# A hybrid encoder kernel on Trainium2: in the chunked delta-rule stage, VectorE does one doubling add after the result ops of the older job, not ahead of them

## The chip, the core and the metric

The kernel is one program on one core of a Trainium2 chip. The core has five engines that run side by side and meet at semaphores: TensorE (PE in the rows, its weight loads PEld), VectorE (DVE), ScalarE (ACT), GpSimd (POOL) and SyncE (SP), which issues DMAs. Each engine takes its own instructions in the order in which they are written. The metric is the device time of one execution in microseconds, lower is better; three runs of the kernel before gave 1784.24 us as their median (1783.65 to 1788.34).

## The reference

One encoder layer over 1024 tokens of width 1024: a projection into three head groups, an output projection, cross-attention into 256 memory tokens, a SwiGLU feed-forward and norms, all in float32. The stage that is changed belongs to the third head group, a bidirectional RWKV-7 mixer with 4 heads of 64, whose state is updated token by token:

```python
def step(S, inp):
    wt, kkt, kat, kt, vt, rt = inp
    S = (S * wt[..., None, :]
         - jnp.einsum('...vk,...k->...v', S, kkt)[..., :, None] * kat[..., None, :]
         + vt[..., :, None] * kt[..., None, :])
    return S, jnp.einsum('...vk,...k->...v', S, rt)

_, y = lax.scan(step, S0, xs)     # xs: both directions, the second one flipped in time
y = jnp.moveaxis(y, 0, 2)
y = y[0] + jnp.flip(y[1], axis=1)
```

## The kernel before

The scan is not run token by token. Time is cut into chunks of 64, two of which make a tile of 128 tokens. For a tile the kernel builds small 64x64 systems, inverts each of them by doubling, and gets from that a transition and an offset per chunk; only the chain over chunks is sequential. A tile in one direction is a job: 8 tiles in 2 directions make jobs 0 to 15 (direction 0 is jobs 0 to 7). A job takes one of three slots in turn (s_G, s_Q, s_LT, s_XQ and s_WU in the rows, with two PSUM banks each), so job g + 3 reuses the slot of job g.

Jobs are pipelined over steps p = 0 to 18. `jobs_at(p)` gives the job that enters (`new`, number p), the one of the step before (`mid`), the one before that (`old`) and the one whose results are ready (`done`). All four engines walk the same steps, each with its own order, written out by hand; nothing reorders it. For a job, the inverse has five rounds, 0 to 4: `new` does rounds 0 and (its first half) 1, `mid` the rest of 1, then 2 and 3, `old` round 4. A round is: TensorE transposes the running inverse Q (two matmuls, L2033) and multiplies it with the coupling block LT that GpSimd made (`xq`, 16 matmuls), ScalarE copies that to SBUF (L919), TensorE multiplies again (`inverse`, 16 matmuls), and VectorE adds the product to Q (`inverse`, L1461, one instruction, called the add here). After round 4 come `wu` and `results` on TensorE (80 small matmuls in `results`), and then `results(old)` on VectorE, four instructions (L1471, L1472, L1473, and L1476 for direction 0 or L1479 for direction 1). `add_y` (L1440) and `chain_step` (L1427, two instructions) belong to `done`.

TensorE's order in a step p, in the parts that matter, is: `xq(old, 4)`, `inverse(mid, 1)`, `gram(new)`, ..., `wu(old)`, `xq(mid, 3)`, `inverse(new, 0)`, `state_out(done)`, `results(old)`, `inverse(mid, 3)`, `xq(new, 1)`, `chain_step(done)`. The `mid` of one step is the `old` of the next, so the `xq(old, 4)` at the head of step p + 1 transposes what the add of `inverse(mid, 3)` of step p has written. `gram(new)` of step p + 1 writes the banks that `results(old)` of step p reads:

```python
def gram(j):                                   # TensorE, L1988
    pe.wait_ge(g_dve[j.i], j.dve0)             # VectorE is through with the slot's last job
...
def xq(j, l):                                  # TensorE, L2036
    pe.wait_ge(g_dve[j.i], j.dve0 + (DVE_Q[l - 1] if l else DVE_SYS))
    inverse_t(j)                               # the two transposes, L2033
```

In steps 1 to 7 VectorE also prepares the inputs of direction 1 piece by piece: `next(inputs1)` issues the next one or two instructions of `second_inputs()` (L1380 to L1419), `DVE_PREP` says how many of them a step has (4 or 5). GpSimd and ScalarE have such extra work in a few steps too. What follows the stage (group norm, output projection and all the rest) starts on every engine with a wait for the last `add_y`.

Of the kernel before, what the change touches and what calls it, by code (L numbers as in the profile page):

```python
# [55 lines left out]
def build(nc, io):  # L56
    out = io["out"]
    ctx = ExitStack()
    with ctx:
# [310 lines left out]
        def jobs_at(p):  # L370

            return [Job(p - age) if 0 <= p - age < 2 * NT else None for age in range(4)]
# [741 lines left out]
        def _(dve):  # L1114
# [327 lines left out]
            def gram(j):  # L1442
                sl = j.slot
                dve.wait_ge(g_pe[j.i], j.pe0 + PE_GRAM)
                for hp in range(2):
                    ins = TT(sl.G[:, :, hp:4:2, 0:2, :].rearrange("p a u r t -> p a u (r t)"),
                             PS[:, (sl.a, sl.b)[hp], :].rearrange("p (a u c) -> p a u c", a=2, u=2),
                             MK[:, j.d, 0:2 * C].unsqueeze(1).unsqueeze(1).broadcast_to([P, 2, 2, 2 * C]), ALU.mult)
                ins.then_inc(g_dve[j.i], 1)

            def system(j):
                sl, q = j.slot, j.slot.Q[:, :, :]
                dve.wait_ge(g_pe[j.i], j.pe0 + PE_SYS)
                link(TT(q.rearrange("p (a h) c -> p a h c", a=2), PS[:, sl.a:sl.b + 1, 0:2 * C].rearrange("p h (a c) -> p a h c", a=2),
                        MK[:, j.d, 2 * C:3 * C].unsqueeze(1).unsqueeze(1).broadcast_to([P, 2, 2, C]), ALU.mult))
                TT(q, q, I64.unsqueeze(1).broadcast_to([P, 4, C]), ALU.subtract).then_inc(g_dve[j.i], 1)

            def inverse(j, l):
                q = j.slot.Q[:, :, :].rearrange("p (a h) k -> p h a k", h=2)
                dve.wait_ge(g_pe[j.i], j.pe0 + PE_Q[l])  # L1460
                TT(q, PS[:, j.slot.a:j.slot.b + 1, 0:128].rearrange("p h (a k) -> p h a k", a=2), q, ALU.add).then_inc(g_dve[j.i], 1)  # L1461
# [20 lines left out]
            for p in range(STEPS):  # L1482
                new, mid, old, done = jobs_at(p)
                extra = DVE_PREP.get(p, 0)
                if mid:
                    inverse(mid, 1)
                if new:
                    gram(new)
                if extra > 4:
                    next(inputs1)  # L1490
                if old:
                    inverse(old, 4)
                if new:
                    system(new)
                if extra:
                    next(inputs1)
                if done:
                    if done.k == 0:
                        chain_first(done)
                    else:  # L1500
                        chain_step(done.d, 2 * done.k)
                if mid:
                    inverse(mid, 2)
                if new:
                    inverse(new, 0)
                if extra:
                    next(inputs1)
                if done:
                    add_y(done)
                if mid:  # L1510
                    inverse(mid, 3)
                if old:
                    results(old)
                if extra:
                    next(inputs1)
                if done and done.k < NT - 1:
                    chain_step(done.d, 2 * done.k + 1)
                if extra:
                    next(inputs1)
# [893 lines left out]
```

## Time and profile before

| what | value |
|---|---|
| median of three runs | 1784.24 us |
| the profiled execution, its own time | 1788.34 us |
| its span in the trace | 1786.5 us |
| TensorE busy | 1695.5 us (95%) |
| VectorE busy | 722.5 us (40%) |
| ScalarE busy | 665.0 us (37%) |
| GpSimd busy | 579.0 us (32%) |
| mean granted TensorE clock | 0.973 of full speed |

The profiled execution is one of the three timed. A row of a timeline gives the start in us from the start of the span, the time in us that the group of equal instructions took, engine, line, operation, what it writes and reads with the shapes, the number of instructions, and in brackets how long the engine was idle ahead of it and which instruction ended that. The ends of matmuls are modelled, as they are pipelined. Instructions of one engine overlap a little in the rows, because the next starts before the last one has drained. The stage goes from about 572 us to 783 us of the span, 12% of it.

### The profile page before, as it was taken

Reading aid. Unit: us, or ns where it says so; the run is one execution under the profiler, and the core shown is the slowest. Engines: PE = TensorE matmul, PEld = TensorE weight load, DVE = VectorE, ACT = ScalarE, POOL = GpSimd, SP = SyncE. Lnnn points to the kernel's source line nnn. Section 1 sums busy time; section 2 is a strip of 40 time slices with the busy share of each in tenths; the row PEclk is TensorE's granted clock in tenths of the full one; section 3 lists DMA queues with packets and bytes.
Section 4 is the critical chain, followed back from the end, with each engine's and each line's share of the span. In section 5 each row is a group of like instructions: output and inputs, shape, how many; then the busy total and the mean of one; then the engine's idle time right before and its main releaser. Section 6 shows DMA issues by size and latency. Waiting matters only on the chain.

```text
span 1786.5 us, 31965 instructions
## 1 busy us (share of the span) xinstructions
PE 1695.5 (95%) x13553; PEld 1398.7 (78%) x13553; DVE 722.5 (40%) x1223; ACT 665.0 (37%) x1244; POOL 579.0 (32%) x529
## 2 busy tenths in 40 slices
PE   6999999999876899989999999999999999999997
PEld 5887878788654677868888878888888888888886
DVE  3105888332165686653532641203303303312316
ACT  5225888423257444442554742211111212121112
POOL 5232663321035543355555013222222222212220
PEclk9999999999868899999999999999999999999999
DMA  6110000210000000016333012111111111111112
GB/s 195 48 64 6 1 1 1 66 48 12 18 1 6 3 4 4 5 43 237 98 107 108 7 42 60 49 53 48 48 47 54 42 47 54 47 42 58 49 42 94
DMA packets 62605, 87.44 MB, mean 49 GB/s; under 512 B 5010, under 2 KB 46128, under 8 KB 62464
## 3 DMA queue, kind: packets, MB, share of 16 engines
q1 hardware_dynamic: 61520, 82.89, 14.5%
q0 software_dynamic: 944, 2.52, 0.5%
q8 instruction: 108, 1.77, 0.4%
q14 instruction: 33, 0.27, 0.0%
HBM read 81.19 MB, written 4.19 MB: 48 GB/s over the span
## 4 chain that ended last, share of the span: by engine, by line
PE 86%; DVE 6%; ACT 4%; DMA 2%; POOL 1%; issue 1%; SPq 0%; ACTq 0%; DVEq 0%
PE PS L1701 13%; PE PS L1704 13%; PE PS L1702 13%; PE PS L1962 6%; PE PS L2333 4%; PE PS L2331 4%; PE PS L2332 4%; PE PS L1714 4%; PE PS L1716 4%; PE PS L1715 4%; PE PS L1806 3%; PE PS L1850 3%; PE PS L2033 2%; PE PS L1842 1%; PE PS L1740 1%
## 5 line engine op out<-in xcount | busy, mean ns | idle before, releaser
L480 POOL TENSOR_TENSOR WL<-RAW,WH 128x512 fp32r<-128x512 f32 x248 | 341.2, 1385 | 837.5 <-ACT WH L656 836.7
L1701 PE MATMUL PS<-HH,WH 128*128 128x512 f32 x1040 | 406.1, 391 | 0.3 <-DVE SM L1150 0.3
L1702 PE MATMUL PS<-HL,WH 128*128 128x512 f32 x1040 | 404.7, 389 | 0.0
L656 ACT ACTIVATE WH<-RAW 128x512 fp32r<-128x512 f32 x248 | 153.5, 631 | 558.8 <-PE PS L1704 275.2
L1704 PE MATMUL PS<-HH,WL 128*128 128x512 f32 x1040 | 325.5, 389 | 0.0
L1704 PEld LDWEIGHTS PS<-HH,WL 128*128 128x128 f32 x1040 | 195.2, 188 | 40.7
L1701 PEld LDWEIGHTS PS<-HH,WH 128*128 128x128 f32 x1040 | 195.3, 188 | 40.5 <-DVE SM L1150 0.4
L1702 PEld LDWEIGHTS PS<-HL,WH 128*128 128x128 f32 x1040 | 195.2, 188 | 40.0
L1651 DVE TENSOR_TENSOR FU<-PS,ACTB 128x512 f32<-128x512 f32 x44 | 27.3, 684 | 456.9 <-PE PS L1704 456.9
L2331 PE MATMUL PS<-WH,AH 128*128 128x512 f32 x352 | 136.9, 389 | 0.0
L2332 PE MATMUL PS<-WL,AH 128*128 128x512 f32 x352 | 136.9, 389 | 0.0
L2333 PE MATMUL PS<-WH,AL 128*128 128x512 f32 x352 | 136.9, 389 | 0.0
L1678 DVE TENSOR_TENSOR X<-PS,X 128x512 f32<-128x512 f32 x160 | 105.3, 686 | 60.1 <-PE PS L2333 60.1
L602 POOL TENSOR_TENSOR s_LT<-s_G,CN 128x256 f32<-128x256 f32 x80 | 60.4, 764 | 121.8 <-PE PS L1962 68.8
L1714 PE MATMUL PS<-WH,HH 128*128 128x512 f32 (+1 forms) x240 | 89.9, 374 | 3.8 <-POOL WL L480 3.8
L1201 DVE CUSTOM_DVE_ANT_0 E__70<-PS,TAB 128x1024 f32<-128x1024 f32 x64 | 78.2, 1225 | 30.8 <-PE PS L1806 29.9
L1716 PE MATMUL PS<-WH,HL 128*128 128x512 f32 (+1 forms) x240 | 88.0, 367 | 0.0
L1715 PE MATMUL PS<-WL,HH 128*128 128x512 f32 (+1 forms) x240 | 87.8, 366 | 0.0
L754 ACT ACTIVATE E__70<-E__70,SM 128x1024 f32<-128x1024 f32 x64 | 73.6, 1151 | 21.0 <-DVE SM L1201 20.8
L919 ACT ACTIVATE s_XQ<-PS 128x512 f32<-128x512 f32 (+1 forms) x80 | 51.2, 640 | 78.0 <-PE PS L1962 78.0
L2333 PEld LDWEIGHTS PS<-WH,AL 128*128 128x128 f32 x352 | 66.1, 188 | 13.7
L2331 PEld LDWEIGHTS PS<-WH,AH 128*128 128x128 f32 x352 | 66.1, 188 | 13.7
(349 smaller groups left out, 2713.1 us busy)
## 6 DMA issues: line engine op xcount, KB each, us to landing
RAW<-in_ffn_w_gu SPq DMA_DIRECT2D x88, 256.0 KB, 2.8
RAW<-in_w_in SPq DMA_DIRECT2D x48, 256.0 KB, 2.7
RAW<-in_ffn_w_down SPq DMA_DIRECT2D x44, 256.0 KB, 2.5
RAW<-in_w_out SPq DMA_DIRECT2D x32, 256.0 KB, 2.8
XT<-in_x SPq DMA_DIRECT2D x8, 512.0 KB, 5.5
X<-in_x SPq DMA_DIRECT2D x8, 512.0 KB, 6.4
RAW<-in_x_wq SPq DMA_DIRECT2D x16, 256.0 KB, 2.7
RAW<-in_x_wkv SPq DMA_DIRECT2D x16, 256.0 KB, 2.6
```

Of the source, the lines that this page charges most:

```text
L480: pool.tensor_tensor(w_low, RAW[:, p % NRAW], w_high.bitcast(F32), ALU.subtract).then_inc(w_lo, 1)
L656: act.activation(split_at(p)[0], RAW[:, p % NRAW], ACT.Copy).then_inc(w_hi, 1)
L1701: pe.matmul(where(ct, i), wh[:, k, c], ah(kt)[:, t0:t0 + n], start=first and starts(ct, i), stop=False, skip_group_check=True)
L1702: pe.matmul(where(ct, i), wh[:, k, c], al(kt)[:, t0:t0 + n], start=False, stop=False, skip_group_check=True)
L1704: mm = pe.matmul(where(ct, i), wl[:, k, c], ah(kt)[:, t0:t0 + n], start=False, stop=last, skip_group_check=True)
L1714: pe.matmul(dst, ah(kt)[:, t], wh, start=start, stop=False, skip_group_check=True)
L1715: pe.matmul(dst, ah(kt)[:, t], wl, start=False, stop=False, skip_group_check=True)
L1716: return pe.matmul(dst, al(kt)[:, t], wh, start=False, stop=last, skip_group_check=True)
L1962: return pe.matmul(dst, lhsT, rhs, start=start, stop=stop, skip_group_check=True)
L2331: pe.matmul(PS[:, bank, :], AH[:, a, t], wh, start=k == 0, stop=False, skip_group_check=True)
L2332: pe.matmul(PS[:, bank, :], AH[:, a, t], wl, start=False, stop=False, skip_group_check=True)
L2333: return pe.matmul(PS[:, bank, :], AL[:, a, t], wh, start=False, stop=k == 1, skip_group_check=True)
```

## The change

On VectorE, `inverse(mid, 3)` moves from ahead of `results(old)` to behind it and behind the `next(inputs1)` that follows. No other engine's code is touched.

```diff
--- before.py
+++ after.py
@@ -1507,12 +1507,12 @@
                     next(inputs1)
                 if done:
                     add_y(done)
-                if mid:
-                    inverse(mid, 3)
                 if old:
                     results(old)
                 if extra:
                     next(inputs1)
+                if mid:
+                    inverse(mid, 3)
                 if done and done.k < NT - 1:
                     chain_step(done.d, 2 * done.k + 1)
                 if extra:
```

The sequences of TensorE, ScalarE, GpSimd and SyncE are the same in both programs. On VectorE, step p = 8 stands like this before, from `add_y` to the mask ops of the next step (KR, BKt: keys of direction 0; YY: the output; g_pe0 to g_pe2: TensorE's semaphore of a slot):

```order
L1440 TENSOR_TENSOR YY<-PS,YY 128x2x128 [waits y_mm]
L1461 TENSOR_TENSOR s_Q<-PS,s_Q 128x2x2x64 [waits g_pe1]
L1471 TENSOR_TENSOR KR<-PS,KR 128x2x128 [waits g_pe0]
L1472 TENSOR_TENSOR BKt<-PS,CN 128x2x128
L1473 TENSOR_TENSOR BKt<-PS,SM 128x2x128
L1476 COPY YY<-PS 128x2x128
L1427 SCALAR_TENSOR_TENSOR KR<-PS,SM,BKt 128x64 [waits c_mm]
L1427 SCALAR_TENSOR_TENSOR KR<-PS,SM,BKt 128x64
L1461 TENSOR_TENSOR s_Q<-PS,s_Q 128x2x2x64 [waits g_pe2]
L1446 TENSOR_TENSOR s_G<-PS,MK 128x4x128 [waits g_pe0]
```

The first L1461 here is the add of `inverse(mid, 3)`, the second that of `inverse(mid, 1)` of step 9. VectorE's step p = 8 in the program after:

```order
L1440 TENSOR_TENSOR YY<-PS,YY 128x2x128 [waits y_mm]
L1471 TENSOR_TENSOR KR<-PS,KR 128x2x128 [waits g_pe0]
L1472 TENSOR_TENSOR BKt<-PS,CN 128x2x128
L1473 TENSOR_TENSOR BKt<-PS,SM 128x2x128
L1476 COPY YY<-PS 128x2x128
L1461 TENSOR_TENSOR s_Q<-PS,s_Q 128x2x2x64 [waits g_pe1]
L1427 SCALAR_TENSOR_TENSOR KR<-PS,SM,BKt 128x64 [waits c_mm]
L1427 SCALAR_TENSOR_TENSOR KR<-PS,SM,BKt 128x64
L1461 TENSOR_TENSOR s_Q<-PS,s_Q 128x2x2x64 [waits g_pe2]
L1446 TENSOR_TENSOR s_G<-PS,MK 128x4x128 [waits g_pe0]
```

The add has moved behind the four ops of `results(old)`. Steps 8 to 16 are alike, but for L1479 in place of L1476 from step 10 on. In step p = 4 (and alike in 2, 3, 5, 6 and 7) VectorE has an op of `second_inputs()` there as well, here an L1402, which the add moves past too:

```order
 L1440 TENSOR_TENSOR YY<-PS,YY 128x2x128 [waits y_mm]
-L1461 TENSOR_TENSOR s_Q<-PS,s_Q 128x2x2x64 [waits g_pe0]
 L1471 TENSOR_TENSOR KR<-PS,KR 128x2x128 [waits g_pe2]
 L1472 TENSOR_TENSOR BKt<-PS,CN 128x2x128
@@ -523,4 +523,5 @@
 L1476 COPY YY<-PS 128x2x128
 L1402 TENSOR_TENSOR B__113<-B__113,ET 128x512
+L1461 TENSOR_TENSOR s_Q<-PS,s_Q 128x2x2x64 [waits g_pe0]
 L1427 SCALAR_TENSOR_TENSOR KR<-PS,SM,BKt 128x64 [waits c_mm]
 L1427 SCALAR_TENSOR_TENSOR KR<-PS,SM,BKt 128x64
```

In step p = 1 VectorE has no `old`, and the add moves past one call of `next(inputs1)` alone, which there is two instructions:

```order
 L1461 TENSOR_TENSOR s_Q<-PS,s_Q 128x2x2x64 [waits g_pe1]
 L1383 SCALAR_TENSOR_TENSOR KR_112<-SCM,KR_112 128x512
+L1386 TENSOR_SCALAR SM<-KR_112 128x16 [waits dve_chain]
+L1388 TENSOR_TENSOR KR_112<-KR_112,SM 128x512 [waits dve_chain]
 L1461 TENSOR_TENSOR s_Q<-PS,s_Q 128x2x2x64 [waits g_pe0,dve_chain]
-L1386 TENSOR_SCALAR SM<-KR_112 128x16
-L1388 TENSOR_TENSOR KR_112<-KR_112,SM 128x512 [waits dve_chain] x2
+L1388 TENSOR_TENSOR KR_112<-KR_112,SM 128x512
 L1461 TENSOR_TENSOR s_Q<-PS,s_Q 128x2x2x64 [waits g_pe1,dve_chain]
```

The second L1461 of this piece is the add; L1386 and the first L1388 now stand ahead of it.

## Rows read from the trace of the kernel before

**Rows 1.** Windows: stretch, its length, busy time of each engine, PEclk, DMA, GB/s
```profile
687.31:763.64 76.33, 76.25 (x2673) 62.65 (x2673) 46.98 (x125) 34.66 (x63) 25.26 (x35) 1.00 0.02 5
640.80:644.20 3.40, 1.58 (x41) 0.97 (x40) 3.40 (x8) 0.95 (x2) 1.24 (x3) 1.00 0.00 0
644.20:647.60 3.40, 3.40 (x64) 2.51 (x68) 2.79 (x7) 1.85 (x4) 1.38 (x2) 0.58 0.02 5
```

**Rows 2.** Timeline of VectorE around the add of step p = 8
```profile
687.31 0.42 DVE L1461 TENSOR_TENSOR s_Q<-PS,s_Q 128x256 f32<-128x256 f32 x1 [1.21 <-PE PS L1962]
...
688.98 0.47 DVE L1427 SCALAR_TENSOR_TENSOR KR<-PS,SM,BKt 128x64 f32<-128x64 f32 x2
```

**Rows 3.** Timeline of TensorE, from the last matmul of results in p = 8
```profile
686.78 0.22 PE L1962 MATMUL PS<-s_G,s_WU 64*64 64x64 f32 x1
686.78 0.45 PE L1962 MATMUL PS<-s_XQ 64*64 64x64 f32 x15
...
688.14 0.44 PE L2033 MATMUL PS<-CN,s_Q 128*128 128x128 f32 x2
...
688.79 0.41 PE L1962 MATMUL PS<-s_XQ 64*64 64x64 f32 x16
689.11 0.67 PE L1962 MATMUL PS<-KR,B__113 64*64 64x128 f32 x16
```

**Rows 4.** Timeline of both engines at the end of step p = 16
```profile
771.93 0.42 DVE L1461 TENSOR_TENSOR s_Q<-PS,s_Q 128x256 f32<-128x256 f32 x1 [1.21 <-PE PS L1962]
...
772.41 0.44 PE L2033 MATMUL PS<-CN,s_Q 128*128 128x128 f32 x2 [0.33 <-DVE s_Q L1461]
```

**Rows 5.** Timelines of VectorE and of TensorE after step p = 5
```profile
652.01 0.42 DVE L1461 TENSOR_TENSOR s_Q<-PS,s_Q 128x256 f32<-128x256 f32 x1 [0.64 <-PE PS L1962]
...
653.68 0.68 DVE L1411 TENSOR_TENSOR KR<-KR,KK 128x512 f32<-128x512 f32 x1
...
655.60 1.28 DVE L1446 TENSOR_TENSOR s_G<-PS,MK 128x512 f32<-128x512 f32 x2
...
652.85 0.44 PE L2033 MATMUL PS<-CN,s_Q 128*128 128x128 f32 x2
...
653.82 1.10 PE L1962 MATMUL PS<-KR,BKt 64*64 64x128 f32 x32
```

**Rows 6.** Timelines of VectorE, GpSimd and TensorE after step p = 4
```profile
639.27 2.15 DVE L1402 TENSOR_TENSOR B__113<-B__113,ET 128x512 f32<-128x512 f32 x1
641.35 0.46 DVE L1427 SCALAR_TENSOR_TENSOR KR<-PS,SM,BKt 128x64 f32<-128x64 f32 x2
...
642.82 1.27 DVE L1446 TENSOR_TENSOR s_G<-PS,MK 128x512 f32<-128x512 f32 x2
...
638.52 2.36 POOL L592 TENSOR_TENSOR B__113<-B__113,KK 128x1024 f32<-128x1024 f32 x1
...
638.54 0.44 PE L2033 MATMUL PS<-CN,s_Q 128*128 128x128 f32 x2
...
639.19 0.41 PE L1962 MATMUL PS<-s_XQ 64*64 64x64 f32 x16
639.42 1.10 PE L1962 MATMUL PS<-KR,BKt 64*64 64x128 f32 x32
```

**Rows 7.** Timelines of VectorE and of TensorE after step p = 1
```profile
597.42 0.52 DVE L1386 TENSOR_SCALAR SM<-KR 128x16 f32<-128x16 f32 x1
597.98 1.42 DVE L1388 TENSOR_TENSOR KR<-KR,SM 128x512 f32<-128x512 f32 x2
...
597.56 0.44 PE L2033 MATMUL PS<-CN,s_Q 128*128 128x128 f32 x2 [0.49 <-DVE s_Q L1461]
...
598.88 1.10 PE L1962 MATMUL PS<-KR,BKt 64*64 64x128 f32 x32 [0.26 <-ACT B__113 L830]
```

**Rows 8.** Timeline of TensorE after step p = 2 and after step p = 7
```profile
614.47 0.70 PE L1962 MATMUL PS<-s_Q,s_LT 64*64 64x64 f32 x16 [0.68 <-POOL s_LT L602]
...
678.22 0.67 PE L1962 MATMUL PS<-KR,B__113 64*64 64x128 f32 x16 [1.21 <-issue]
```

## The prediction

> **What bounds the kernel now.** I count the stage in steps p, as the code does; the add is VectorE's op of L1461 for `inverse(mid, 3)`, which starts at 652.01 us in p = 5, at 687.31 in p = 8 and at 771.93 in p = 16 [rows 2, 4, 5].
>
> First I read the windows by stage. From p = 8 to p = 15 TensorE is busy for 76.25 of 76.33 us at the full clock [rows 1], and VectorE for 46.98. Seven steps fit in, 10.9 us each, so a hole that is newly made in TensorE's row there is added to the time. Before p = 8 VectorE is the busier engine and TensorE waits at places.
>
> Second, the timelines of both engines at one steady step. VectorE finishes `add_y`, sits idle for 1.21 us, and at 687.31 does the add, 0.08 us after the last matmul that makes its input (686.78 + 0.45 = 687.23). The four ops of `results(old)` follow, then `chain_step` at 688.98 [rows 2]. That looks like a hole to fill, since the input of `results(old)` was complete at 686.78 + 0.22 = 687.00 [rows 3], 0.23 us sooner.
>
> Third, who needs these two. TensorE runs `inverse(mid, 3)`, `xq(new, 1)`, `chain_step`, and then, as the first work of the next step, the two transposes (L2033, 688.14) of the block that the add writes. Two groups later comes `gram(new)`, at 689.11, which reuses the slot that `results(old)` reads [rows 3]. The add is therefore needed first, at 688.14, and now ends 0.41 us before (687.31 + 0.42 = 687.73). `results(old)` is needed second: its last op started at 688.98 - 0.33 = 688.65, and its end some 0.4 us later, about 689.05, is just ahead of the start of `gram`.
>
> **The change, part by part.** No instruction is added or removed on any engine, one add moves behind four ops, and in p = 1 to 7 also behind one op of `second_inputs()`. In p = 0 and 17 to 18 nothing moves. 16 steps have a `mid`, p = 1 to 16.
>
> *p = 8 to 15.* Five starts from 687.31 to 688.98 make 0.334 us an op [rows 2]. Now `results(old)` starts at 687.31 - 0.23 = 687.08, the add at 687.08 + 4 x 0.334 = 688.42, and it ends at 688.84. TensorE starts about 0.06 us after such an end (771.93 + 0.42 = 772.35, then 772.41 [rows 4]), at 688.90 instead of 688.14: a stall of 0.76 us. What is queued behind it on TensorE is everything: `inverse(mid, 1)`, `gram`, the transposes of the keys. One thing comes back: `gram` waited for `results(old)` a little, since a group of 16 such matmuls that nobody holds is followed after 0.23 us (639.42 - 639.19 [rows 6]) and here after 0.32 (688.79 to 689.11 [rows 3]). So 0.76 - 0.09 = 0.67 us a step. The seven steps p = 8 to 14 give 4.7 us. In p = 15 there is no `gram` behind: 0.76.
>
> *p = 16.* TensorE already waits here for the add, [0.33 <-DVE] at 772.41 [rows 4]. The add moves by 4 x 0.334 - 0.23 = 1.11 us, and the last chain of `xq`, `inverse`, `wu`, `results` hangs on it: 1.11.
>
> *p = 3, 5, 6.* One op of `second_inputs()` goes ahead as well. At p = 5: the add starts at 652.01 - 0.23 + 1.34 + 0.60 = 653.72 (0.60 is the 0.68 us of the op at 653.68 less the 0.08 by which ops in a row overlap, 0.42 long and 0.334 apart), ends at 654.14, and TensorE goes on at 654.20 instead of 652.85, 1.35 late, 1.26 at `gram`. But here VectorE got to the mask ops of the next step (L1446) only at 655.60; TensorE's `gram` ended at 654.92, and will end at 656.18, so that VectorE starts 0.06 later, at 656.24: 0.64 us of the 1.26 is seen [rows 5]. Steps 3 and 6 have the same rows, at p = 3 with a longer extra op: 3 x 0.64 = 1.9.
>
> *p = 4.* VectorE has no idle ahead of the add here, so `results(old)` takes its place, and the extra op (L1402) starts one op sooner, 639.27 - 0.33 = 638.94. That op took 2.15 us at 639.27, and a GpSimd op of 2.36 us lay beside it from 638.52 to 640.88 [rows 6]. If it always takes its 2.08 us from start to start, the add starts at 641.02, TensorE resumes 0.48 us later, at 641.50 instead of 638.54, `gram` ends at 640.52 + 2.96 = 643.48, and VectorE's mask op starts at 643.54 instead of 642.82: 0.72. If it is held until the GpSimd op ends, it is over no sooner than before, and the add starts at 641.35: 1.05. Lower bound 0.7, upper 1.1; I take 1.0, as this row is the only one of its kind that is that long and its end follows GpSimd's. The Trainium skill says of this (SBUF — State Buffer, section "SBUF: two separate sides") that a VectorE op with two SBUF inputs and a GpSimd op exclude each other on a shared port for the whole instruction; by that rule the term is 1.05, without it 0.72, and the trace leans to the rule with 2.15 us against 0.68 for an op of the same size at 653.68 [rows 5].
>
> *p = 1.* No `old` yet, two small ops go ahead (L1386 and one L1388): 0.56 + 0.71 = 1.27 us. TensorE waits for the add at 597.56 already, but at 598.88 it waited for ScalarE. The way from the transposes to `gram` takes 0.65 us (688.14 to 688.79 [rows 3]) and 0.23, so it would have been ready at 598.44, and 0.44 is slack [rows 7]: 0.83.
>
> *p = 2 and 7.* After p = 2 the next release of TensorE is GpSimd's, at 614.47 [rows 8]. TensorE's stall is large, since a scan goes ahead of the add, yet GpSimd's work doesn't move with it: 0.1, at worst 0.5. After p = 7 TensorE stood at `gram` for 1.21 us, for a small VectorE op that now comes 0.2 us sooner [rows 8]; the stall of 1.35 fills that hole: 0, between -0.2 and +0.2.
>
> *The clock.* In 640.80 to 644.20 TensorE was busy for 1.58 us and in the next 3.40 us its granted clock was 0.58, that is mostly 1.2 GHz [rows 1]. One such stretch costs at most 0.42 x 3.4 = 1.4 us. The holes made here have 0.7 us in the steady part; the forecast keeps the present number of slow stretches (bounds: one fewer, -1.4; three more, +4.3).
>
> *Sum:* 0.83 + 0.1 + 1.9 + 1.0 + 0 + 4.7 + 0.76 + 1.11 = 10.4 us. On the profiled execution (1788.34, span 1786.5) that is 1798.7. That execution was the slowest of the three shown, 4.1 above the median, with nothing to say that the stage caused it, so I put the sum on the median: 1784.24 + 10.4 = **1794.6**. What follows the stage starts from the last `add_y` on all engines, so nothing later can take it back.
>
> **The rivals.**
> *Not slower.* VectorE is the bound, and its idle 1.21 us is now partly used. Then each of the 15 steps with both jobs ends 0.23 us sooner: -3.5, 1780.8. For it: VectorE is fully busy from 640.80 to 644.20 [rows 1]. It decides if TensorE needs the doubling add at least 1.1 us after it is now done; at p = 8 it has 0.41 us [rows 2, 3], so this fails at each step. Chance 0.03.
> *The early steps hide it.* Only p = 8 to 16 counts, as the waits of p = 1 to 7 swallow the rest: 4.7 + 0.76 + 1.11 = 6.6, 1790.8. For it: TensorE was busy for 1.58 of 3.40 us there [rows 1]. Against: the slack was subtracted above. Chance 0.09.
> *More slow clock early.* The holes of 1.3 to 3.3 us in p = 1 to 6 drop the clock in up to three more steps: +4.3, 1798.9. For it: the row of 0.58. Against: the hole of 1.21 us after p = 7 [rows 8] was followed by none, the clock being 1.00 from p = 8 on. Chance 0.14.
> *The clock alternates in every step.* 14 stretches of 1.4: +20, 1814.6. The 76 us at full clock have no hole of this kind, so rows neither show nor exclude it; holes up to 1.2 us without a fall speak against it. Chance 0.03. The Trainium skill speaks for this one: TensorE: Matmul & The Clock Gate, section "A second HAM failure mode: psum-queue depth-cycling", tells of a kernel in which short idles between groups of matmuls came often enough for the clock to swing. No row of this trace shows that.
>
> **How the numbers follow.** The forecast has 0.71, with its own range 1791.5 to 1797.5 (terms of p = 1, 2, 4 and 7 at their bounds, one slow stretch either way, half a microsecond for the median itself). The four rivals have the other 0.29. The range of eight in ten takes in the early-hiding case at the low end and the three stretches at the high end: 1790 to 1800. A measurement of this kernel can tell about 0.3%, 5.4 us, so 1789.6 is the border. All cases but the first rival lie above it, the second by 1.2 us only, half a term: slower 0.94, within 0.05, faster 0.01.
>
> **What would show it.** In the new trace TensorE's transposes L2033 at the head of each step carry an idle of about 0.7 us released by DVE L1461, and a steady step lasts 11.55 us instead of 10.89. VectorE's idle before L1461 there falls from 1.21 us to nothing, and a shorter one of about 1.0 us stands before L1471. From the start of p = 8 to that of p = 15 it is 81.0 us instead of 76.3. Wrong would be a steady step that stays at 10.9 us, TensorE's next wait being on `gram`, or a granted clock under 1.00 between p = 8 and 15.

## The result

The changed kernel takes 1804.86 us (median of 4 runs, 1802.16 to 1805.86), the kernel before 1784.63 in the same comparison: ratio 1.0107, interval 1.0089 to 1.0126. The forecast was 1794.6 with a range of 1790 to 1800. The direction was right, the time was 10 us too low and outside the range.

The comparison flatters the kernel before. In the later comparisons, up to both_fill, it ran 97 more times between 1782.5 and 1797.9, median 1789.2 (17 more beside combo have 1788.1). The four times above, of which three are those that I started from, lie for the most part at the low end of that spread. One further execution of it, 2150.4 us, has no trace and is left out. A second comparison of the changed kernel gave 1804.5 (6 runs, 1799.5 to 1808.0) beside 1789.5, ratio 1.0078, interval 1.0059 to 1.0097. So the change costs 14 to 15 us, not 20, where the forecast's sum had 10.4.

### The profile page after: what moved, and what is told of

It is laid out like the page before. It is cut to its first block, busy times and chain, and to the rows that moved or that the text cites. A ratio compares the mean times of both kernels' runs of the same rounds, so it can differ in the third digit from the quotient of the medians.

```text
span 1798.0 us, 31966 instructions
## 1 busy us (share of the span) xinstructions
PE 1692.0 (94%) x13553; PEld 1396.2 (78%) x13553; DVE 720.9 (40%) x1223; ACT 666.0 (37%) x1244; POOL 577.1 (32%) x529
## 4 chain that ended last, share of the span: by engine, by line
PE 86%; DVE 7%; ACT 4%; DMA 1%; issue 1%; POOL 1%; SPq 0%; ACTq 0%; DVEq 0%
PE PS L1701 13%; PE PS L1704 13%; PE PS L1702 13%; PE PS L1962 7%; PE PS L2333 4%; PE PS L2331 4%; PE PS L2332 4%; PE PS L1714 4%; PE PS L1716 4%; PE PS L1715 4%; PE PS L1806 3%; PE PS L1850 3%; PE PS L2033 2%; PE PS L1842 1%; PE PS L1740 1%
## 5 line engine op out<-in xcount | busy, mean ns | idle before, releaser
L602 POOL TENSOR_TENSOR s_LT<-s_G,CN 128x256 f32<-128x256 f32 x80 | 60.4, 763 | 132.5 <-PE PS L1962 67.8
L1714 PE MATMUL PS<-WH,HH 128*128 128x512 f32 (+1 forms) x240 | 89.6, 373 | 3.1 <-POOL WL L480 3.0
L2332 PEld LDWEIGHTS PS<-WL,AH 128*128 128x128 f32 x352 | 66.1, 188 | 13.7
L2331 PEld LDWEIGHTS PS<-WH,AH 128*128 128x128 f32 x352 | 66.1, 188 | 13.7
```

Source lines behind the costliest of these rows:

```text
L1714: pe.matmul(dst, ah(kt)[:, t], wh, start=start, stop=False, skip_group_check=True)
L2331: pe.matmul(PS[:, bank, :], AH[:, a, t], wh, start=k == 0, stop=False, skip_group_check=True)
L2332: pe.matmul(PS[:, bank, :], AH[:, a, t], wl, start=False, stop=False, skip_group_check=True)
```

## The profile after, against the rows of before

Windows of the changed kernel, one for each of the steps p = 1 to 5 (each from the first mask op L1446 of a step to that of the next) and one for p = 8 to 14. Columns are length, busy time of TensorE, its weight load, VectorE, ScalarE and GpSimd, then the granted clock, the DMA share and GB/s.

```profile
583.26:596.17 12.91, 9.87 (x243) 6.94 (x244) 9.23 (x14) 5.97 (x9) 4.25 (x5) 0.96 0.01 3
596.17:610.47 14.30, 11.89 (x353) 9.31 (x354) 10.43 (x18) 4.93 (x9) 12.23 (x11) 0.86 0.01 3
610.47:628.83 18.36, 14.53 (x377) 12.02 (x378) 12.06 (x23) 9.18 (x13) 10.24 (x10) 0.78 0.01 3
628.83:642.90 14.07, 11.10 (x385) 9.16 (x386) 11.07 (x23) 4.96 (x9) 10.72 (x9) 0.98 0.01 4
642.90:655.27 12.37, 10.81 (x385) 8.88 (x385) 9.46 (x22) 7.80 (x13) 3.60 (x5) 1.00 0.02 4
...
679.85:760.18 80.33, 75.33 (x2681) 61.81 (x2676) 47.44 (x124) 34.69 (x63) 25.23 (x35) 1.00 0.02 5
```

In the steady part TensorE was busy for 76.25 of 76.33 us [rows 1], and is now for 75.33 of 80.33, at the full clock both times. The new 4 to 5 us are holes, and nothing else changed there. In p = 1 and 2 the granted clock is below 1; before, it was 1.00 in both. Before, it was low in p = 3 (0.69) and p = 5 (0.87) instead. Length times missing clock, summed over p = 1 to 7, is about 6.8 us in this trace as in that of before; in after_again it is 8.4, in early 9.8.

Timelines of VectorE and of TensorE in step p = 8 (the bracket is the engine's idle time just before the row and what released it):

```profile
687.93 0.42 DVE L1471 TENSOR_TENSOR KR<-PS,KR 128x256 f32<-128x256 f32 x1 [0.98 <-PE PS L1962]
688.27 0.41 DVE L1472 TENSOR_TENSOR BKt<-PS,CN 128x256 f32<-128x256 f32 x1
688.60 0.41 DVE L1473 TENSOR_TENSOR BKt<-PS,SM 128x256 f32<-128x256 f32 x1
688.93 0.41 DVE L1476 COPY YY<-PS 128x256 f32<-128x256 f32 x1
689.26 0.42 DVE L1461 TENSOR_TENSOR s_Q<-PS,s_Q 128x256 f32<-128x256 f32 x1
...
688.67 0.40 PE L1962 MATMUL PS<-KR,BKt 64*64 64x64 f32 x8
689.74 0.44 PE L2033 MATMUL PS<-CN,s_Q 128*128 128x128 f32 x2 [0.67 <-DVE s_Q L1461]
```

This is the predicted picture of [rows 2] and [rows 3]: the idle of 1.21 us ahead of the add is now 0.98 ahead of L1471, and TensorE stands for 0.67 us until the add is done. The sum had 0.76 for this wait. The steady step is 11.49 us instead of 10.89; seven of them differ by 4.0 us.

The last step with an add, p = 16, answers to [rows 4]:

```profile
779.10 0.44 PE L2033 MATMUL PS<-CN,s_Q 128*128 128x128 f32 x2 [1.42 <-DVE s_Q L1461]
```

0.33 us of waiting has become 1.42, 1.09 more; the forecast had 1.11.

Step p = 5, for [rows 5], VectorE, GpSimd and TensorE:

```profile
651.58 0.42 DVE L1476 COPY YY<-PS 128x256 f32<-128x256 f32 x1
651.91 0.97 DVE L1411 TENSOR_TENSOR KR<-KR,KK 128x512 f32<-128x512 f32 x1
652.80 0.41 DVE L1461 TENSOR_TENSOR s_Q<-PS,s_Q 128x256 f32<-128x256 f32 x1
...
655.27 1.29 DVE L1446 TENSOR_TENSOR s_G<-PS,MK 128x512 f32<-128x512 f32 x2 [0.45 <-PE PS L1962]
...
651.61 0.72 POOL L602 TENSOR_TENSOR s_LT<-s_G,CN 128x256 f32<-128x256 f32 x1 [2.32 <-PE PS L1962]
...
653.27 0.44 PE L2033 MATMUL PS<-CN,s_Q 128*128 128x128 f32 x2 [1.56 <-DVE s_Q L1461]
```

The mechanism is the forecast's: the stall is passed on through `gram`, and VectorE then waits 0.45 us for it. But the op L1411 now starts while GpSimd's L602 is running (651.61 to 652.33) and takes 0.97 us where it took 0.68, so that it ends 0.55 us after L602. Its place in time had changed, and I had priced it at its old duration.

Step p = 4, for [rows 6]:

```profile
638.12 2.38 DVE L1402 TENSOR_TENSOR B__113<-B__113,ET 128x512 f32<-128x512 f32 x1
640.42 0.41 DVE L1461 TENSOR_TENSOR s_Q<-PS,s_Q 128x256 f32<-128x256 f32 x1
...
637.62 2.34 POOL L592 TENSOR_TENSOR B__113<-B__113,KK 128x1024 f32<-128x1024 f32 x1
...
640.89 0.44 PE L2033 MATMUL PS<-CN,s_Q 128*128 128x128 f32 x2 [2.97 <-DVE s_Q L1461]
```

L1402 ends at 640.50, 0.54 us after GpSimd's op; before, it ended 0.54 after it as well (641.42 and 640.88). Against GpSimd's op it started 0.25 us earlier and took 0.23 us longer. The Trainium skill's rule (SBUF — State Buffer, section "SBUF: two separate sides"), under which the term was 1.05 instead of 0.72, is borne out: the step takes 14.07 us instead of 13.01 (14.00 in both_fill, at the full clock).

Steps p = 1 and p = 2 are where the picture differs, TensorE at [rows 7] and [rows 8]:

```profile
593.78 0.44 PE L2033 MATMUL PS<-CN,s_Q 128*128 128x128 f32 x2 [1.90 <-DVE s_Q L1461]
...
594.66 1.46 PE L1962 MATMUL PS<-KR,BKt 64*64 64x128 f32 x32
596.05 1.11 PE L2007 MATMUL PS<-CN,BKt 128*128 128x128 f32 x4
...
607.76 0.44 PE L2033 MATMUL PS<-CN,s_Q 128*128 128x128 f32 x2 [2.41 <-DVE s_Q L1461]
...
608.64 1.78 PE L1962 MATMUL PS<-KR,BKt 64*64 64x128 f32 x32
610.35 1.11 PE L2007 MATMUL PS<-CN,BKt 128*128 128x128 f32 x4
```

Behind these two holes of 1.9 and 2.4 us the clock falls to its low level (granted 0.50 from 596 to 598 and from 610 to 612 us), and it falls on `gram` (1.46 and 1.78 us for what takes 1.10, row 598.88 in [rows 7]) and on the transposes of the keys (1.11; 0.66 at 655.14, at the full clock). VectorE waits for that `gram`. A long hole alone does not bring the low clock about: the holes of 2.97 us in p = 4 and 1.56 in p = 5 left it at 0.98 and 1.00 in this trace. The forecast had let the number of slow stretches stand; I had not asked where they would lie.

The end of the stage, from the last add (L1461 in p = 17) to the end of the last `add_y`, has the same instructions in both programs. Windows of it, before and changed:

```profile
774.49:783.04 8.55, 4.67 (x152) 3.78 (x148) 3.93 (x13) 0.98 (x2) 0.00 (x0) 1.00 0.01 4
781.18:791.36 10.18, 6.54 (x152) 5.67 (x148) 3.93 (x13) 0.98 (x2) 0.00 (x0) 0.75 0.01 3
```

It takes 1.6 us longer, at a granted clock of 0.75 instead of 1.00; in after_again and late it is 10.5 us. The forecast priced nothing here. The low clock stands behind the new wait of 1.42 us at L2033, but that this wait brings it about is not shown: one_op, in which the add moves by 0.10 us only, has 10.5 too.

Last, the work behind the stage, which the prediction left out. TensorE in the kernel before, then in the changed one:

```profile
783.10 3.70 PE L2143 MATMUL PS<-YY,CN 128*128 128x512 f32 x8 [0.53 <-DVE YY L1440]
787.76 3.70 PE L2143 MATMUL PS<-CIN,CN 128*128 128x512 f32 x8 [0.96 <-DVE CIN L1524]
792.02 4.37 PE L1869 MATMUL PS<-CN,SQY 128*128 128x2 f32 x32 [0.55 <-ACT SQY L976]
796.25 0.77 PE L1714 MATMUL PS<-WH,HH 128*128 128x512 f32 x1
```

```profile
791.42 6.24 PE L2143 MATMUL PS<-YY,CN 128*128 128x512 f32 x8 [0.53 <-DVE YY L1440]
797.49 3.60 PE L2143 MATMUL PS<-CIN,CN 128*128 128x512 f32 x8
801.98 5.74 PE L1869 MATMUL PS<-CN,SQY 128*128 128x2 f32 x32 [0.89 <-ACT SQY L976]
807.59 0.77 PE L1714 MATMUL PS<-WH,HH 128*128 128x512 f32 x1
```

No instruction differs here, yet from L2143's start to the first L1714 it is 13.15 us before and 16.17 now, since the first group (L2143) took 6.24 us instead of 3.70 and L1869 5.74 instead of 4.37, with a granted clock of 0.61 from 791.42 to 798 us. The profiled execution is 1800.18 us, 12 more than that of before (1788.34); the stage itself, from the first mask op to the end of its last `add_y`, is 13.5 us longer (209.5 to 223.0: 6.1 in p = 1 to 7, 4.0 in p = 8 to 14, 3.5 from p = 15 on), this stretch 3.0, and the first part of the kernel happened to be 5.2 shorter, by its granted clock (0.89 instead of 0.84 from 400 to 560 us).

## The experiments

All were timed beside the kernel before on the same chip. The times in us that the first expectations name stand on a kernel before of 1784.6; it had 1789.1 beside them, so the differences are what to compare. Extra lines shift the line numbers: L2033 of before is L2035 or L2037 in some runs, L2143 is L2153. The length of each step, read from the starts of L1446, in us:

| kernel | p=1 | 2 | 3 | 4 | 5 | 6 | 7 | 8 to 14 | ratio (interval) |
|---|---|---|---|---|---|---|---|---|---|
| before | 11.59 | 13.18 | 16.59 | 13.01 | 12.78 | 11.39 | 12.39 | 76.34 | 1 |
| changed | 12.91 | 14.30 | 18.36 | 14.07 | 12.37 | 12.39 | 12.59 | 80.33 | 1.0107 |
| changed again | 13.16 | 14.37 | 17.09 | 15.53 | 13.56 | 12.38 | 12.60 | 80.34 | 1.0078 (1.0059 to 1.0097) |
| early | 13.09 | 14.39 | 17.06 | 15.36 | 12.37 | 13.34 | 14.14 | 77.35 | 1.0059 (1.0038 to 1.0080) |
| late | 11.59 | 13.17 | 16.59 | 13.00 | 12.78 | 11.39 | 12.39 | 81.37 | 1.0032 (1.0016 to 1.0049) |
| early_res | 11.60 | 12.93 | 15.58 | 13.03 | 11.38 | 11.49 | 12.16 | 78.66 | 0.9990 (0.9976 to 1.0004) |
| early_extra | 13.06 | 13.45 | 15.80 | 12.34 | 10.95 | 11.46 | 11.82 | 78.06 | 0.9990 (0.9973 to 1.0007) |
| after_fill | 12.54 | 13.11 | 17.14 | 14.01 | 12.56 | 12.42 | 12.60 | 82.51 | 1.0055 (1.0038 to 1.0072) |
| both_fill | 12.53 | 13.10 | 17.16 | 14.00 | 12.40 | 12.45 | 12.86 | 83.56 | 1.0043 (1.0027 to 1.0060) |

**before_again: the kernel before, once more.** 

> The kernel before, once more, for a second trace. The first trace of it lasted 1788.3 us and the median of its runs is 1784.6. If executions differ by where TensorE's clock falls (the first trace has 0.50 to 0.54 in 572.8 to 586.4 and 0.5 in 613.6 to 623.8), this trace lasts about 1784 us and has fewer or shorter stretches under 1.00 up to the end of the scan stage, with the steps p = 8 to 15 at 10.9 us as before. If the 4 us were something else (DMA, a longer launch), the stretches are the same.

1788.49 us, and each step of p = 1 to 7 within 0.02 us of the first trace. The expectation of another clock pattern was a miss: the same steps (p = 3 at 0.69, p = 5 at 0.87) are slow again.

**early and late: the change in p = 1 to 7 alone, and in p = 8 to 16 alone.**

```
early:                                   late:
-                if mid:                 -                if mid:
+                if mid and p >= 8:      +                if mid and p < 8:
                     inverse(mid, 3)                          inverse(mid, 3)
                 (results, extra)                         (results, extra)
+                if mid and p < 8:       +                if mid and p >= 8:
+                    inverse(mid, 3)     +                    inverse(mid, 3)
```

> The add is moved in steps p = 1 to 7 alone, and stands where it did from p = 8 on. The prediction's terms for these steps give 0.83 + 0.1 + 1.9 + 1.0 = 3.9 us: 1788.5. If the holes made in TensorE there also lower its granted clock (the trace after has 0.69 to 0.81 in p = 1 to 4), the time is 6 us or more above before, 1790.5 to 1794, and the steps p = 1 to 4 together are at least 4 us longer than before.

> The add is moved in steps p = 8 to 16 alone. Order alone: 7 steps of 0.6 (as measured in the trace after), 0.76 and 1.11, together 6.1 us: 1790.7. If the clock is what made the rest, the time is above that only by what falls at the end of the stage (granted 0.60 at 783.6 to 787.0 and 0.5 at 804 to 811 in the trace after): up to 3 us more, 1793.7. If early and late parts add up to the whole +20 us, neither part alone can be near these sums, and late would be at 1796 or more.

late: 1794.62 us, 5.7 above the kernel before, where the forecast's terms for p = 8 to 16 give 6.6. early: 1798.85, 10.5 above by its ratio, where the terms give 3.9. So the later part came out near its sum and the early one did not. The two add up to 16, against 14 to 19 for the whole. That late came out near is partly luck: its steady steps take 5.0 us more than before instead of 4.7, and the end of the stage is 2.0 longer, which the sum had at nothing, so that its trace is 8.8 us longer from p = 1 on.

**one_op and late_three: the dose.** The add stands behind one of the four ops of `results` (p = 2 to 16), or behind three of them (p = 8 to 16).

```
                 TT(g, rm[:, :, :, 0, :], g, ALU.add)
+                if between:          # one_op: here; late_three: two ops on
+                    between()
```

> The add is put behind the first of the four result ops (L1471) in steps p = 2 to 16, and stands as before in p = 1. By the order theory what counts is how much later the add ends than TensorE needs it: it had 0.41 us ahead, less 0.06 for the semaphore, and now moves by 0.334 - 0.23 = 0.10 us, so TensorE doesn't wait in the steady steps, and gram, which waited 0.09 us for the results, is released 0.23 us sooner: the steady step is 10.80 us instead of 10.89, and the whole is between -2 and 0 us against before, 1782.6 to 1784.6. If any op ahead of the add costs (a theory by which the position itself matters, not the time), it is slower by 0.3 us a step, about +5.

> In p = 8 to 16 the add goes behind three of the four ops of results(old), and nothing changes in p = 1 to 7. The steady step was 10.89 us with the add first, about 10.9 behind one op, 11.49 behind four. By the forecast's working (0.334 us an op, a slack of 0.41 + 0.23 us, 0.09 back at gram): 0.334 less than with four, 11.16 us. If the step were set by something that all orders but the first share, it would be 11.49 here too.

one_op took 1787.56 us, ratio 0.9988 (0.9973 to 1.0003): no loss, and a gain that is not told from nothing. Its steady steps are 10.85 us at best, not the expected 10.80, and some have gaps (11.47, 11.53). late_three, one execution, has undisturbed steady steps of 11.16 to 11.18 us, as its expectation worked out; with the add first they are 10.89, behind four ops 11.49. The fourth op costs 0.32 us and one op costs nothing: the slack, and 0.33 us for an op behind it, are shown in the length of the step.

**after_again: the changed kernel beside the parts.** 

> The changed kernel once more, timed beside the kernel before on this chip. The parts run alone gave +10.5 us (p = 1 to 7) and +5.7 (p = 8 to 16), together 16. Theory A, the parts add up: ratio 1.009, 15 to 18 us above the kernel before. Theory B, the first difference of 20 us came from a kernel before that was timed in a low moment (1784.6 against 1789.1 later): 10 to 13 us, as the forecast's sum had it (10.4). The steady steps are 11.49 us again under both.

Ratio 1.0078, between the two expectations: the parts add up within the intervals (14 by this ratio, 19 by the first, 16 by the parts), and 10 us lies just outside the interval (10.6 to 17.4).

**early_res: in p = 2 to 7 the add behind `results`, but ahead of the extra op.** 

> In p = 2 to 7 the add goes behind results(old) but stays ahead of the op of second_inputs(); p = 1 and p = 8 to 16 are as before. It divides the +10.5 us of the early part. If the loss is the four ops of results(old) (1.11 us a step, in six steps, less what is hidden): +4 to +7 us. If it is the op of second_inputs() that goes ahead (0.6 to 2.1 us a step, and it drags a GpSimd op along): 0 to +3 us here, and the rest, 7 us or more, comes with that op.

```
-                if mid:
+                if mid and p >= 8:
                     inverse(mid, 3)
                 if old:
                     results(old)
+                if mid and p < 8:
+                    inverse(mid, 3)
                 if extra:
```

0.9990 (0.9976 to 1.0004): it costs 0.7 us at most, where 4 to 7 had been expected if the four ops were the loss. Its trace has TensorE waiting for the add behind each of p = 2 to 7 (0.93, 0.67, 0.72, 0.67, 0.67 and 0.67 us), and the steps no longer for it, but for 0.1 in p = 6: `gram` is late by less than VectorE's own lead.

**early_extra: the extra op first, then the add, then `results`.** 

> In p = 1 to 7 the op of second_inputs() goes ahead of the add, and results(old) behind both; p = 8 to 16 are as before. The add behind results(old) alone cost nothing (0.999), behind both it cost 10.5 us. Theory threshold: VectorE is the bound of these steps and absorbs a late gram up to about 0.7 us; one op ahead of the add (0.6 us, 2.1 in p = 4) stays under that but in p = 4, as the four ops alone (1.1 us) did, and only both together pass it: 0 to +3 us. Theory that the loss is the order of the op of second_inputs() itself, by what it drags along on GpSimd: +6 us or more here too.

```
-                if mid:
+                if mid and p >= 8:
+                    inverse(mid, 3)
+                if extra:
+                    next(inputs1)
+                if mid and p < 8:
                     inverse(mid, 3)
                 if old:
                     results(old)
-                if extra:
-                    next(inputs1)
```

0.9990 as well (0.9973 to 1.0007). Four ops alone cost nothing, the extra op alone costs nothing, both together cost 10.5 us (early, 7 to 14 by its interval). That is a threshold, as the forecast's subtraction at p = 5 had it (1.26 us late at `gram`, 0.64 of it seen), and it speaks against a loss that the extra op brings along by itself on GpSimd. Single steps do change: p = 1, which is as in early, is 1.5 us longer than before, p = 4 and 5 are 0.7 and 1.8 shorter.

**early_567: the change in p = 5, 6 and 7 alone.** 

> The add goes behind results(old) and the op of second_inputs() in p = 5, 6 and 7 alone. The forecast had 0.64, 0.64 and 0 for these: +1.3 us. The traces of the changed kernel have 12.38 us for a full-clock step p = 5 or 6 where 11.38 would be free of any wait: +1.0 each and some 0.3 in p = 7, together +2.3. If most of the +10.5 us sat here: +5 or more; otherwise p = 1 to 4 carry some 6 to 8 us, where the forecast had 2.6.

```
-                if mid:
+                if mid and p not in (5, 6, 7):
                     inverse(mid, 3)
                 (results, extra)
+                if mid and p in (5, 6, 7):
+                    inverse(mid, 3)
```

1792.78 us, ratio 1.0020 (1.0000 to 1.0040), 3.6 us with an interval of 0 to 7. It holds both 1.3 and 2.3 and cannot tell them apart; in its trace p = 6 and 7 are 1.0 and 0.2 us longer than before. The greater part of the early loss seems to be left for p = 1 to 4.

**after_fill: the changed kernel with matmuls in the new holes.** 

> The changed kernel, with five extra matmuls (128 x 128, result unused) on TensorE at the end of p = 1 to 6, where it waits for the moved add. They fill about 1.1 us of the wait and change no order of the real work. If the early loss is granted clock lost behind the new holes: 3 to 6 us faster than the changed kernel, and no window of p = 1 to 7 under 0.9. If it is the waits themselves: within 2 us of the changed kernel, and the slow windows may go without any gain.

```
+                if 1 <= p <= 6:
+                    for _ in range(5):
+                        pe.matmul(PS[:, FRONT, 0:128], ID, ID, start=True, stop=True, ...)
```

The result of these matmuls is unused; they are called filler below. 1800.82 us, 4 less than the changed kernel beside it, though the intervals of the two ratios (1.0038 to 1.0072 here, 1.0059 to 1.0097 there) overlap. p = 1, 2 and 4 are at the full clock, as windows of its successor both_fill show:

```profile
586.11:598.64 12.53, 10.80 (x253) 7.90 (x254) 9.23 (x14) 5.97 (x9) 4.25 (x5) 1.00 0.01 3
598.64:611.74 13.10, 11.52 (x363) 9.26 (x363) 11.01 (x18) 4.93 (x9) 11.41 (x10) 1.00 0.01 4
611.74:628.90 17.16, 14.77 (x387) 12.27 (x388) 11.89 (x24) 9.17 (x13) 11.28 (x11) 0.80 0.01 3
628.90:642.90 14.00, 12.36 (x395) 10.20 (x395) 11.50 (x22) 4.96 (x9) 10.67 (x9) 1.00 0.02 4
```

The same steps took 12.91 to 13.16, 14.30 to 14.39 and 14.07 to 15.53 us in the three traces without filler. The clock's part of these steps is the difference, 0.4 to 0.6, 1.2 to 1.3 and 0.1 to 1.5 us. (In early, p = 6 and 7 are slow as well, at 0.92 and 0.86.) What is left against before is the wait alone: 0.94, -0.08 and 0.99 us, where the forecast had 0.83, 0.1 and 1.0. Of its expectation's window under 0.9 one stayed, in p = 3, where the hole is another one.

**tail_fill, before_tail: matmuls in the waits of p = 18, in the changed kernel and in the one before.**

```
+                if p == STEPS - 1:
+                    fill(6, FRONT)       # ahead of chain_step; 2 ahead of state_out, 2 at the end
```

> The changed kernel, with ten extra matmuls (results unused) on TensorE in the last step of the stage, p = 18, where it waits 1.8, 0.6 and 0.5 us; nothing real is moved. In the traces of the changed kernel the 8 matmuls of L2143 behind the stage took 6.2 to 6.8 us and those of L1869 5.2 to 5.7, against 3.70 and 4.4 to 4.7 before; from the last add_y to the first matmul of the next projection it is 16.2 us against 13.2 to 13.7. If the holes of that last step set the clock there: 16.2 becomes 13 or less and the time 2 to 4 us shorter. If not: 16.2 stays, and the time is that of the changed kernel.

> The kernel before with the ten extra matmuls in p = 18 alone. It tells whether they pay only where the changed order had lost the clock: two traces of the kernel before had 13.2 and 13.7 us behind the stage, and 12.4 is to be had, so 0 to 1 us under the kernel before. If the stretch behind the stage is slow in many of its executions too (its times spread over 15 us): 2 to 3 us under it, and the filler in the changed kernel corrected nothing that the change had done.

TensorE behind the stage in tail_fill:

```profile
796.67 3.70 PE L2153 MATMUL PS<-YY,CN 128*128 128x512 f32 x8
801.34 3.70 PE L2153 MATMUL PS<-CIN,CN 128*128 128x512 f32 x8 [0.97 <-DVE CIN L1524]
805.48 3.73 PE L1869 MATMUL PS<-CN,SQY 128*128 128x2 f32 x32 [0.44 <-ACT SQY L976]
809.08 0.70 PE L1714 MATMUL PS<-WH,HH 128*128 128x512 f32 x1
```

16.2 us became 12.4, and the changed kernel's ratio 1.0051 (1.0032 to 1.0070), 1798.66 us. But the kernel before gains as well: 1785.75, ratio 0.9980 (0.9962 to 0.9997), 0.5 to 6.8 us. Its trace has 12.7 us there, where the two traces of before have 13.2 and 13.7, which alone would be a gain of 0.5 to 1.0. So other executions of before may have the stretch slow; no trace of it does. early_res, as fast as before, has it slow (16.2). The difference of the two kernels with this filler is 12.9 us, against 14 to 15 without. I had taken the stretch for a loss of 3 us by the change, and this control takes 1 to 2 of them back.

**both_fill: both fillers in the changed kernel.** 

> The changed kernel with both fillers: five extra matmuls at the end of p = 1 to 6 and ten in p = 18 (results unused). Alone, the one left 1800.8 us with a slow clock behind the stage (16.2 us to the next projection), the other 1798.7 with a slow clock in p = 1, 2 and 4. If clock is what the forecast lacked: both together lie at the forecast's waits, 10 us above the kernel before or less (7 to 10), with 12.4 us behind the stage and 12.5, 13.1 and 14.0 us in p = 1, 2 and 4. If the fillers gain nothing together beyond the better one: 10 to 12 us.

1798.52 us, ratio 1.0043: 7.7 us above before, within the expected 7 to 10, but no better than tail_fill alone, and 12.8 above before_tail, which was timed beside it. So it does not show that the waits of the forecast are all that is left at the full clock. Against tail_fill its trace has won 5.3 us in p = 1 to 7 and lost 2.9 in p = 8 to 14. There TensorE stood once in each of the seven steps inside or at the end of a group of `results` (0.19 us, then 0.58 to 0.71) for nothing that the profile shows:

```profile
700.75 0.21 PE L1962 MATMUL PS<-s_G,s_WU 64*64 64x64 f32 x1 [0.65 <-issue]
```

The two traces of before, the two of the changed kernel and that of tail_fill have no such gap in p = 8 to 14; late has none either; the other ten have one to four. They are one reason for 82 or 83 us where seven undisturbed steps take 80.3. The extra matmuls may add to them; this was not tried apart.

**best_fill: early_res with matmuls in p = 0 to 6 and 18.** 

> The version that might beat both: in p = 2 to 7 the add behind results(old) only, p = 8 to 16 as before, and extra matmuls (results unused) in TensorE's waits: 5 and 7 in p = 0, 3 at the end of p = 1 to 6, 10 in p = 18. At equal mean granted clock the early order cost nothing; the filler can win what slow stretches cost in p = 0 to 7 and behind the stage, 8 to 14 us of slow clock in the traces, of which at most half is worth time: 3 to 7 us under the kernel before. If the clock is not tied to these waits: within 1 us of it.

1788.99 us, ratio 0.9993 (0.9978 to 1.0008): a miss. The granted clock rose from a mean of 0.976 to 0.982 and p = 0 to 7 took 100.3 us instead of 105.8, but steady steps with gaps (12.25 us, 11.52) and the stretch behind the stage (14.6) gave it back in the trace. A clock that is kept up in waits is not time won.

**combo: early_extra, one_op for p = 8 to 16, and the filler of p = 18.** 

> The parts that cost nothing or gained, together: in p = 1 to 7 the op of second_inputs() first, then the add, then results(old); in p = 8 to 16 the add behind the first of the four ops of results(old); and the ten extra matmuls in p = 18 (results unused). Alone they stood at 0.9990, 0.9988 and 0.9980. If they add: 0.996, 6 to 8 us under the kernel before. If the first two are no gain at all, as their intervals allow: 0.998, 3 to 4 us under it.

1782.51 us (12 runs, 1778.20 to 1784.97), ratio 0.9965, interval 0.9949 to 0.9981. It beats both kernels, at the low edge of what was expected (5.6 us by the medians, 6.3 by the ratio). Since before_tail alone has 0.9980, the two orders are worth some 2 to 3 us together by the ratios, which their intervals do not tell from nothing. Its undisturbed steady steps are 10.75 to 10.77 us, shorter than the 10.89 of before.

## Why the prediction was wrong

**The mechanism was right.** TensorE, not VectorE, needs the add at the head of each step; the hole on VectorE was no slack. The signs of the steady part came as named: 0.67 us of idle at L2033 released by L1461, 11.49 us a step (forecast 11.55), 0.98 us ahead of L1471 (about 1.0), 80.3 us for seven steps (81.0), granted clock 1.00.

**The waits, term by term** (forecast, measured at the full clock): p = 1 0.83, 0.94; p = 2 0.1, -0.1; p = 4 1.0, 1.0; p = 5 and 6 0.64 each, 1.0 each (12.37 and 12.39 against 11.38 in early_res and 11.39 in before); p = 7 0, 0.2 (for its hole of 1.21 us the row names "issue", not the small VectorE op that I named); p = 8 to 14 4.7, 4.0; p = 15 and 16 1.87, 1.84 (the add of p = 16 starts 18.05 us behind the mask op of p = 15 instead of 16.21). p = 3 cannot be had free of the clock. With 1.0 for it, as for its likes p = 5 and 6, which is an assumption, the sum is 10.9, and the forecast had 10.4. Two waits were mis-sized: that of p = 5 and 6 by 0.35 us each, 0.3 of which is what L1411 takes longer beside GpSimd, and the steady one, 0.57 us a step where I had 0.67. That the two errors nearly cancel, +0.7 and -0.7 us, is luck. One reading was wrong without effect on the sum: before p = 8 VectorE is not the busier engine (70.5 us against 81.1 of TensorE in p = 1 to 7 of before). The rival that VectorE gains, the one in which the early steps hide everything, and the alternating clock in the steady part are refuted: the change costs time, early costs 10.5 us, and the steady clock is 1.00 with a hole of 0.67 us in each step. For the last one the Trainium skill had spoken (TensorE: Matmul & The Clock Gate, "A second HAM failure mode: psum-queue depth-cycling"); holes of this kind do not bring it about here.

**What failed, first step: "I put the sum on the median: 1784.24".** Three runs gave 1783.65 to 1788.34, and I allowed half a microsecond for it. The kernel's usual time is 1789.2 (median of 97 runs), with a standard deviation of 3.6. This is 5.0 of the 10.3 us by which the time was missed. The changed kernel had 1804.86 in the first comparison and 1804.5 in the second, so it was the times of before that lay low, and not the whole comparison. I had also argued the profiled 1788.34 away as the slow one of three; it was the ordinary one.

**Second step: "the forecast keeps the present number of slow stretches", the clock put at nothing.** In the traces p = 1 to 7 together are longer than before by 6.1 us (changed kernel), 7.8 (after_again) and 8.8 (early). The waits above make 5.0 of it, with the assumed 1.0 for p = 3, so 1.0, 2.7 and 3.8 are left for the clock. The slow time had hardly grown in the first of them (6.8 us both times); it had moved onto `gram`, for which VectorE waits. The end of the stage, in which nothing moved, adds 1.6 to 2.0 us at a clock of 0.66 to 0.75. For the changed kernel that is 2.6 to 4.7 us where the forecast had 0. With the 5.0 of the base and 0.5 of the waits it makes 8.1 to 10.2 of the 10.3 us.

The rival "more slow clock early", to which I gave 0.14, comes nearest: holes of 1.9 to 3.0 us were being made next to the rows in which a short idle stretch was followed by 0.58. But it expected more slow steps, where the first trace has the same slow time in other places, and the end of the stage was in no rival.

A second way to the same number is weaker. Each run lists its mean granted clock. Over 229 executions of all kernels but combo, with a level for each kernel, the time falls by 0.99 us (standard error 0.05) for each 0.001 of it. At equal clock the changed kernel stands 12.0 us above the one before (11.8 and 12.2 in the two comparisons, each to about 0.9), late 4.5, early 8.1; and the changed kernel's clock is lower by 0.0027, 0.973 for 0.976, which is 2.7 us more. This is an estimate from a correlation, not a price: late's 4.5 lies under its own waits of 5.8, and by the same line best_fill, whose clock was raised by filler, stands 5.9 us above the kernel before and took the same time.

**A third step, in part settled: "nothing later can take it back".** Nothing did, but later work could add: the stretch behind the stage has 13.2 or 16.2 us by the clock that it meets. By the control before_tail a part of these 3 us, 1 to 2, does not belong to the change; whether the change makes the slow case more frequent is open, since a run without a profile doesn't show it.

What is left open: p = 3 was never seen at the full clock in the changed order, so how its part divides between wait and clock was not measured; why the clock fell behind some holes and not behind others (p = 4 has 0.98 in one trace of the changed kernel and 0.87 in the other) is not shown; and late has 5.7 us by its ratio (2.9 to 8.8) where its trace is 8.8 longer from p = 1 to the end of the stage. For early the two agree, 10.5 and 10.3.

## What to carry to other kernels

Look for the consumer that needs a result first; an idle engine ahead of an op may be the price of serving it at once. When a change makes holes in front of a matmul group that others wait for, price that group and the end of the chain at the low clock as well, and cost every moved op by what GpSimd runs beside it in its new place. Before a few microseconds are forecast, get the spread of the base from more than three runs: here it (a standard deviation of 3.6 us) was wider than all of the terms but one.

## What the runs showed of the hardware

- One core alone, undisturbed, spreads by 15 us (0.8%), and the time goes with the mean granted clock of the execution: the correlation in the kernel before alone is -0.79, that is six tenths of the variance.
- A VectorE op with two SBUF inputs that started in the middle of a GpSimd op ended 0.54 to 0.55 us after it, all three times looked at: L1402 twice, and L1411, which took 0.97 instead of 0.68 us beside a GpSimd op of 0.72.
- Ten unused matmuls in three waits of 0.5 to 1.8 us made the stretch behind the stage 12.4 us instead of 16.2 in the changed kernel and 12.7 instead of 13.2 and 13.7 in the one before, which gained 0.2% of the whole. In best_fill, with the same ten, it was 14.6.
- Between execution and span there are 1.85 us in before, late, early_res, early_extra and early_567, but 2.13 to 2.16 in the changed kernel, early and the filled versions of the changed kernel. I have no cause for these 0.3 us.
- Work that no edit touched was slower by where the clock fell: the end of the stage has 8.55 to 9.0 us in the six traces that leave p = 8 to 16 alone and have no filler in p = 18, and 9.5 to 10.5 in every trace in which the add moves there. With filler in p = 18 and the old order it has 9.75 (before_tail) and 8.56 (best_fill), so the order alone does not set it.
